# Rows of 512 tokens for the normed pair and y, and the second block's product of p ahead of its gate

## The chip, the cores and the metric

The kernel is one program on one core of a Trainium2 chip. The metric is the device time of one execution in microseconds (us), lower is better. TensorE multiplies, VectorE and ScalarE do the elementwise work, GpSimd a little of it, SyncE's queue issues nearly all loads of weights.

## The reference

Three model blocks in sequence act on 512 tokens of 1024 features (the first block on 528, since 16 meta tokens stand in front). Cut to the part that is written in another order, the end of the second block, and to the shape that most of the program has, a normed x times a weight:

```python
        hf = rmsnorm(x, norm_ffn[i])
        up = causal_dwconv(hf @ w_up[i], ffn_dw_w[i], ffn_dw_b[i])
        gate, val = jnp.split(up, 2, axis=-1)
        x = x + (jax.nn.gelu(gate) * val) @ w_down[i]

        pg = jax.nn.sigmoid(rmsnorm(x, norm_ple[i]) @ w_ple_gate[i])
        x = x + pg * (p[i] @ w_ple[i])
    return rmsnorm(x, norm_final)
```

p has 256 features per token; w_ple_gate is 1024 by 1024, w_ple 256 by 1024.

## The kernel before

Features lie on the 128 partitions, tokens along the row, so a tensor of 1024 features is 8 tiles of [128, tokens]. Products are in single precision by way of pairs: a tensor is split into a high part, rounded to the matmul's format, and the rest, the low part. One tile of a weight (128 by 128) times one tile of x takes three matmuls at L278: whi by x_hi, whi by x_lo, wlo by x_hi, with 512 columns each, and a weight load of 128 columns ahead of each.

`chain` runs a list of `Job`s, a product each, over weight slabs of up to 8 tiles. For slab s SyncE's queue loads `wbuf`, ScalarE makes `whi` (L297), VectorE subtracts to `wlo` (L395), TensorE multiplies (L278); with `ring=3` there are three buffers of each. A slab's load waits until the slab three earlier was subtracted, and ScalarE's copy waits until TensorE has used that one. Each engine takes its instructions in the order in which they are written. In turn s ScalarE and VectorE first make the slab s + 2 and then evict the tile that ended with slab s (`evict`). Norms are folded in: where a job has a `fold`, its eviction also writes the normed pair of the new x (`folded`: L315 high part, L428 low part) and squares of x (L318, L322); where two norms follow each other, both sums of squares are kept, and GpSimd adds them up (L241). The scale of a normed product is applied at its eviction, after the statistics of the sums (two matmuls with ones, a square root, a reciprocal).

The normed pair `h` is two tensors of 8 rows of T1 = 528 tokens (2112 bytes a row). The first block's projections read all 528 tokens (`rwkv_project` L679 and `qkv` L1440, in halves of 264 columns; the gates' 512 late tokens at L278). Everything later uses `half_pair`, 512 tokens of each row of 528. y, the output of the first block's recurrence, has rows of 528 too. Other operands of L278 (`gates`, `arena`, `u_hi`, `u_lo`, `o`) have rows of 512 tokens, 2048 bytes.

The second block ends with a chain of three jobs: `ffn_down_2` (kind "add", 22 tiles of weights for each of 8 output tiles, in slabs of 7, 7 and 8), `ple_gate_2` (kind "sigmoid", 8 output tiles of one slab of 8), `ple_2` (kind "sum", 8 output tiles of one slab of 2 tiles, so 6 matmuls each; its fold writes the third block's pair with both norms). Ahead of it runs the chain of `ffn_up_2`, after it the first chain of the third block.

Of the kernel before, what the change touches and what calls it, by code (L numbers as in the profile page):

```python
# [58 lines left out]
class Job:  # L59
# [3 lines left out]
    def __init__(self, w, x, kind, dst=None, gate=None, other=None, raw=None, source=None, scaled=False, fold=None):  # L63
# [46 lines left out]
def chain(nc, ones, jobs, T, norm, pending=None, ring=4, side=None, loads=(), taps=None, restore=None, ahead=None,  # L110
# [12 lines left out]
    for j, n in tiles_:  # L123
# [3 lines left out]
        sig_no.append((sig_no[-1] if sig_no else 0) + (job.kind == "sigmoid" and job.scaled))  # L127
        value_no.append((value_no[-1] if value_no else 0) + (job.kind in ("sum", "join") or (job.kind == "ffn" and n % 2 == 1)))
# [42 lines left out]
    with stage(nc) as s_:  # L171
# [35 lines left out]
        with nc.Block() as block:  # L207
# [82 lines left out]
            def _(act):  # L290
# [33 lines left out]
                def evict(s, t):  # L324
# [5 lines left out]
                    elif job.kind == "sigmoid":  # L330
                        act.wait_ge(evicted_d, by_dve[t])
                        copy(job.dst[n], job.dst[n], ACT.Sigmoid).then_inc(sig_done, 1)
                    elif job.kind == "join":
# [17 lines left out]
                    elif job.fold is not None:  # L351
                        act.wait_ge(*((value, value_no[t]) if job.kind == "sum" else (evicted_d, by_dve[t])))
# [36 lines left out]
            def _(dve):  # L389
# [47 lines left out]
                def evict(s, t):  # L437
# [16 lines left out]
                    elif job.kind in ("sum", "join"):  # L454
# [15 lines left out]
                    if job.fold is not None:  # L470
                        last = first[j] + job.N * len(job.groups)
                        if job.kind == "sum" and n > 0:
                            folded(job.fold, n - 1, job.dst[n - 1], last)
                        if job.kind != "sum" or n == job.N - 1:
                            folded(job.fold, n, job.dst[n], last)
# [370 lines left out]
def rwkv_tiles(nc, c, y, fac_scr, early, chunk_decay):  # L846
# [10 lines left out]
    with stage(nc) as s:  # L857
# [48 lines left out]
        with nc.Block() as block:  # L906
# [296 lines left out]
            def _(dve):  # L1203
# [73 lines left out]
                def outputs(i):  # L1277
                    dve.wait_ge(sr_copied, i + 1)
                    yv = y[:, i, RM:T1].rearrange("p (w a t) -> p w a t", w=W, a=2)
# [40 lines left out]
class HeadsNorm:  # L1320
# [14 lines left out]
    def pe_mean(self, pe, i):  # L1335
        if i < 8:
            if i > 0:
                pe.wait_ge(self.cen_ready, i)
            self.nc.tensor.matmul(self.mean[:], self.c["mean64"][:], self.y[:, i, T1 - T2:T1], start=True, stop=True).then_inc(self.mean_ready, 1)
# [35 lines left out]
    def dve(self, dve, t):  # L1375
        TT, TS, STT = self.nc.vector.tensor_tensor, self.nc.vector.tensor_scalar, self.nc.vector.scalar_tensor_tensor
        i, cen, var, y = t // 3, self.cen, self.var, self.y[:, t // 3, T1 - T2:T1]
# [2008 lines left out]

def half_pair(h):

    return tuple([part[:, k, 0:T2] for k in range(8)] for part in h)
# [19 lines left out]
def first_block(nc, a, x, h, ones_ident, both, far, near, norm, ahead, to_next, second):  # L3409
# [8 lines left out]
    with ExitStack() as m:  # L3418
        c = {**a, **ones_ident, **{n: resident(nc, m, n, a[n].shape) for n in CONSTANTS[1]}}
        y, y_lo = overlaid(nc, m, "y", [P, 8, T1])  # L3420
        mp = m.enter_context(ExitStack())
        p_next = mp.enter_context(nc.sbuf_tensor("p_next", [P, 3, T1], F32, side="right"))
        with ExitStack() as m2:
            decay = resident(nc, m2, "chunk_decay", [P, 8, RN + 1])
            early = y[:, 2:8, :].rearrange("p k t -> p (k t)")[:, 0:5 * (RM + 48 + RN * RC)].rearrange("p (f t) -> p f t", f=5)
            with ExitStack() as m3:
                first = resident(nc, m3, "first", [P, 8, P])
                opening(nc, a, c, both, x, h, far, near, first)
                rwkv_project(nc, c, a["w_rwkv_1"], a["w_qkv_1"], p_next, first, h, factors, early, decay, bonus, gate)
            rwkv_tiles(nc, c, y, factors, early, decay)  # L3430
        o, o_lo = overlaid(nc, m, "o", [P, 8, T2])
        with ExitStack() as m2:
            p = tile_list(p_next) + tile_list(act(m2, "p", 21))
            qkv(nc, a["w_qkv_1"][3:], h, p[3:], HeadsNorm(nc, c, y, bonus, gate))
            diff_attention(nc, c, p, o, a["subln_1"], h[0][:, 0, :], ahead, a["w_gates_1"])
        mp.close()
        late = slice(T1 - T2, T1)
        y, y_lo, o, o_lo, x = (tile_list(ap) for ap in (y[:, :, late], y_lo[:, :, late], o, o_lo, x[:, :, late]))
# [5 lines left out]
        jobs = [Job(a["w_gates_1"], tuple(tile_list(part[:, :, late]) for part in h), "sigmoid", dst=gates),  # L3444
# [10 lines left out]
def second_block(nc, a, x, h, ones_ident, far, near, kept, linear, norm, ahead, pending, to_next, second):  # L3455
# [8 lines left out]
    with ExitStack() as m:  # L3464
# [33 lines left out]
        plain, u_hi = (tile_list(t) for t in overlaid(nc, m, "u_hi", [P, 22, T2]))  # L3498
        u = (u_hi, high(m, "u_lo", 22))
        with ExitStack() as m1:  # L3500
            p, p_lo = overlaid(nc, m1, "p", [P, 2, T2])
            chain(nc, ones, [Job(a["ffn_up_2"], now, "ffn", dst=u, scaled=True)], T2, norm, ahead=ahead.take(), following=a["ffn_down_2"], pending=to_ffn, ring=3, taps=c["ffn_taps"],
                  loads=[(p[:], a["p_2"])])
# [4 lines left out]
            ple_gate, p_pair, ps = plain[0:8], (u_hi[8:10], tile_list(p_lo)), tile_list(p)  # L3508
# [5 lines left out]
    return third  # L3514


def third_block(nc, a, x, h, ones_ident, early, kept, linear, norm, ahead, pending, out):

    norms, xs, now = ones_ident["norms"], tile_list(x), half_pair(h)
# [3 lines left out]
    with ExitStack() as m:  # L3523
        branches = [overlaid(nc, m, name, [P, 4, T2]) for name in ("o_m", "o_l", "o_d")]
        o_m, o_l, o_d = (plain for plain, _ in branches)
# [27 lines left out]
        parts = [tile_list(plain) for plain, _ in branches]  # L3553
        pairs = [(rounded[24 + 4 * (n % 2):28 + 4 * (n % 2)], tile_list(low)) for n, (_, low) in enumerate(branches)]
# [11 lines left out]
def program(nc, a, out):  # L3566

    with ExitStack() as memory:
        common = {n: resident(nc, memory, n, a[n].shape) for n in CONSTANTS[0]}
        x, h = resident(nc, memory, "x", [P, 8, T1]), resident_pair(nc, memory, "h", [P, 8, T1])  # L3570
# [7 lines left out]
        to_third = Fold(half_pair(h), both[:, 1, :], 1e-6, norms[:, INNER[1], :], 1e-6)  # L3578
        far = nc.dram_tensor("bias_by_distance", (8, P, 640), F32).ap()
        near = nc.dram_tensor("bias_by_residue", (8, 16, 62), F32).ap()  # L3580
        kept, linear = ExitStack(), ExitStack()
# [176 lines left out]
```

## Time and profile before

| what | us |
|---|---|
| median of 3 runs (3595.03, 3599.8, 3618.14) | 3599.8 |
| the profiled execution, its own time | 3602.74 |
| its span | 3600.9 |
| TensorE busy (93% of the span) | 3335.8 |
| VectorE busy (55%) | 1968.1 |
| ScalarE busy (35%) | 1273.7 |
| GpSimd busy (10%) | 369.9 |

The mean granted TensorE clock is 0.953 of full speed. Start times are in us from the span's start. A matmul's record lasts about 0.39 us and overlaps the next one's; how often one starts is read from the count in a stretch.

### The profile page before, as it was taken

How to read it: one execution, taken by the hardware profiler on the slowest of the kernel's cores; microseconds unless marked ns; L12 is line 12 of the kernel's file. 1: busy time of each engine (PE TensorE's matmuls, PEld its weight loads, DVE VectorE, ACT ScalarE, POOL GpSimd, SP SyncE). 2: the span in 40 equal slices, each digit the busy share in tenths (PEclk: the TensorE clock that was granted, in tenths of full speed). 3: DMA queues.
4: the chain of work that ended last, by engine and by line, in shares of the span. 5: the costliest groups of instructions: out<-in, count | busy, mean ns of one | idle time of the engine just before them, and what ended most of it. 6: DMA issues, size and time to landing. Idle time of an engine off the chain costs nothing. (4 is left out here: it accounts for less than half of the span.)

```text
span 3600.9 us, 57034 instructions
## 1 busy us (share of the span) xinstructions
PE 3335.8 (93%) x24148; PEld 2744.3 (76%) x24148; DVE 1968.1 (55%) x3021; ACT 1273.7 (35%) x2188; POOL 369.9 (10%) x292
## 2 busy tenths in 40 slices
PE   7998999999999999889999999979599889999998
PEld 6987988866888888666777887857587587878886
DVE  4985564565355344486545775356736545464343
ACT  4552323255334233215433443234312324333232
POOL 2322230020000001009300000020100020000000
PEclk9998998999999999998999999989799799999999
DMA  4432112201222222420122222312022003232221
GB/s 150 149 133 69 35 33 101 71 7 50 97 92 95 95 94 89 130 76 27 48 85 93 98 94 92 107 63 77 12 95 85 1 2 117 76 105 100 94 94 65
DMA packets 99317, 287.83 MB, mean 80 GB/s; under 512 B 19594, under 2 KB 23818, under 8 KB 97016
## 3 DMA queue, kind: packets, MB, share of 16 engines
q1 hardware_dynamic: 92528, 269.27, 22.5%
q10 hardware_dynamic: 6536, 14.91, 1.6%
q8 instruction: 192, 3.15, 0.4%
q14 instruction: 61, 0.50, 0.0%
HBM read 264.22 MB, written 19.89 MB: 79 GB/s over the span
## 5 line engine op out<-in xcount | busy, mean ns | idle before, releaser
L278 PE MATMUL acc<-h_hi,whi 128*128 128x512 f32 x1992 | 796.5, 400 | 48.4 <-DVE wlo L505 36.5
L278 PE MATMUL acc<-h_hi,wlo 128*128 128x512 f32 x1992 | 790.6, 397 | 0.0
L278 PE MATMUL acc<-h_lo,whi 128*128 128x512 f32 x1928 | 769.2, 399 | 0.0
L278 PEld LDWEIGHTS acc<-h_hi,whi 128*128 128x128 f32 x1992 | 378.9, 190 | 147.8 <-DVE wlo L505 38.7
L395 DVE TENSOR_TENSOR wlo<-wbuf,whi 128x1024 fp32r<-128x1024 f32 (+3 forms) x277 | 321.8, 1162 | 276.2 <-ACT whi L297 273.7
L278 PEld LDWEIGHTS acc<-h_hi,wlo 128*128 128x128 f32 x1992 | 378.9, 190 | 87.1
L278 PEld LDWEIGHTS acc<-h_lo,whi 128*128 128x128 f32 x1928 | 366.3, 190 | 87.8 <-issue 2.9
L297 ACT ACTIVATE whi<-wbuf 128x1024 fp32r<-128x1024 f32 (+3 forms) x277 | 274.4, 991 | 315.6 <-PE acc L278 290.2
L278 PE MATMUL acc<-arena_round,whi 128*128 128x512 f32 x736 | 236.7, 392 | 4.8 <-DVE arena_round L461 4.8
L395 DVE TENSOR_TENSOR wlo<-ahead,whi 128x1024 fp32r<-128x1024 f32 (+3 forms) x132 | 154.6, 1171 | 140.6 <-ACT whi L297 139.9
L297 ACT ACTIVATE whi<-ahead 128x1024 fp32r<-128x1024 f32 (+3 forms) x132 | 131.4, 995 | 172.0 <-PE acc L278 166.5
L241 POOL TENSOR_TENSOR sums<-sums,sqx 128x512 f32<-128x512 f32 x28 | 38.6, 1400 | 1273.4 <-ACT sqx L318 1273.4
L278 PEld LDWEIGHTS acc<-arena_round,whi 128*128 128x128 f32 x736 | 139.4, 190 | 34.9 <-DVE arena_round L461 5.6
L278 PE MATMUL acc<-arena_round,wlo 128*128 128x512 f32 x416 | 162.9, 391 | 0.0
L679 PE MATMUL acc<-h_hi,whi 128*128 128x264 f32 x480 | 141.2, 294 | 7.5 <-POOL wlo L667 7.5
L278 PE MATMUL acc<-gates_round,whi 128*128 128x512 f32 x384 | 140.0, 392 | 3.0 <-DVE gates_round L461 1.8
L467 DVE TENSOR_TENSOR x<-acc,x 128x512 f32<-128x512 f32 x64 | 44.2, 691 | 175.2 <-PE acc L278 175.2
L679 PE MATMUL acc<-h_lo,whi 128*128 128x264 f32 x480 | 136.8, 285 | 0.0
L679 PE MATMUL acc<-h_hi,wlo 128*128 128x264 f32 x480 | 136.8, 285 | 0.0
L278 PE MATMUL acc<-gates_round,wlo 128*128 128x512 f32 x320 | 124.9, 390 | 0.0
L338 ACT ACTIVATE val<-tmp 128x512 f32<-128x512 f32 x64 | 40.5, 633 | 216.6 <-DVE tmp L463 216.6
L1440 PE MATMUL acc<-h_hi,whi 128*128 128x264 f32 x336 | 102.8, 306 | 2.5 <-DVE wlo L1480 2.5
(764 smaller groups left out, 6412.5 us busy)
## 6 DMA issues: line engine op xcount, KB each, us to landing
wbuf<-in_mlp_out SPq DMA_DIRECT2D x46, 512.0 KB, 3.3
wbuf<-in_mlp_in SPq DMA_DIRECT2D x45, 512.0 KB, 3.2
wbuf<-in_w_gates SPq DMA_DIRECT2D x38, 512.0 KB, 3.3
wbuf<-in_ffn_up SPq DMA_DIRECT2D x29, 512.0 KB, 3.2
wbuf<-in_w_qkv SPq DMA_DIRECT2D x22, 512.0 KB, 3.4
rwkv_factors<-factors SPq DMA_DIRECT2D x8, 1320.0 KB, 4.6
ahead<-in_mlp_in SPq DMA_DIRECT2D x19, 512.0 KB, 3.3
wbuf<-in_w_rwkv SPq DMA_DIRECT2D x18, 512.0 KB, 5.6
```

What stands on the lines that cost most here:

```text
L241: nc.gpsimd.tensor_tensor(sums[q][:], sums[q][:], sqx[q][:], ALU.add).then_inc(both_summed, 1)
L278: mm = nc.tensor.matmul(acc[t % NB][:, 0:T], wt[s % ring][:, k - a, :], xt, start=(kx == 0 and q == 0), stop=(kx == job.K - 1 and q == 2))
L297: copy(whi[s % ring][:, 0:size(s), :], wbuf[s % ring][:, 0:size(s), :], ACT.Copy).then_inc(hi_ready, 1)
L338: copy(val[t % 2][:], tmp[t % 2][:], ACT.Square)
L395: TT(wlo[s % ring][:, 0:size(s), :], wbuf[s % ring][:, 0:size(s), :], whi[s % ring][:, 0:size(s), :].bitcast(F32), ALU.subtract).then_inc( ...
L467: TT(job.dst[n], ps, job.other[n], ALU.add).then_inc(evicted_d, 1)
L679: mm = nc.tensor.matmul(acc[n % 2][:, hf, 0:H], wt[n % R][:, kx, :], xt[:, kx, at], start=(kx == 0 and q == 0), stop=(kx == 7 and q == 2))
L1440: mm = nc.tensor.matmul(acc[n % NB][:, h, 0:H], wt[n % R][:, k, :], xt[:, k, h * H:(h + 1) * H], start=(k == 0 and q == 0), stop=(k == 7 a ...
```

## The change

1. **Rows.** `NormedPair` lays out each part of the pair twice over the same bytes: `by_meta`, rows of 528 for the first block's projections, and `late`, rows of 512. y has rows of 512. The pads of the two tensors make both parts' late rows start at byte 480 modulo 2048, and what is allocated behind them moves along. The third block gets a pair of its own (`third_pair`, first 16 rows of the u tensor), and its three branch outputs lie where h was.
2. **Order.** The chain that ends the second block runs `ple_2` first (kind "copy", ScalarE evicts to `from_p`), then `ffn_down_2`, then `ple_gate_2` with a new kind "gated": VectorE scales the tile, ScalarE takes the sigmoid, VectorE multiplies with `from_p` and adds x, and the fold follows. The kind "sum" with a fold is no longer used.

Starts of the operands of L278 as they are allocated, in bytes modulo 2048, high part / low part:

| operand pair | before | after |
|---|---|---|
| half pair h, rows 0 to 7 | 1952, 2016, 32, ... 352 / 416, 480, ... 864 | 480 / 480 |
| late tokens of `by_meta` (gates of the first block) | 2016, 32, ... / 480, 544, ... | 2016, 32, ... / 544, 608, ... |
| y | 1504 / 1056, 1120, ... 1504 | 480 / 480 |
| diff_out (h row, o) | 1952, 2016, ... / 1504 | 480 / 480 |
| u | 992 / 992 | 480 / 480 |
| arena (third MLP, w_out) | 992 / 992 | 480 / 480 |
| arena by o_m, o_l, o_d | 992 / 992 | 480 / 1952 |
| attention output of the second block | 1472 / 736 | 960 / 736 |
| conv, joined gates of the second block | 1472 / 1472 | 960 / 960 |

```diff
+class NormedPair:
+    def __init__(self, nc, memory):
...
+        names = ((f"h_hi_{nc.next_id()}", 8 * T1 + 16), (f"h_lo_{nc.next_id()}", 8 * T1 + 368))
+        flat = [memory.enter_context(nc.sbuf_tensor(name, [P, n], F32R)) for name, n in names]
+        self.by_meta = tuple(t[:, 0:8 * T1].rearrange("p (k t) -> p k t", t=T1) for t in flat)
+        starts = (144, 0)
+        self.late = tuple(t[:, at:at + 8 * T2].rearrange("p (k t) -> p k t", t=T2) for t, at in zip(flat, starts))
...
-    return tuple([part[:, k, 0:T2] for k in range(8)] for part in h)
+    return tuple([part[:, k, :] for k in range(8)] for part in h.late)
...
-        y, y_lo = overlaid(nc, m, "y", [P, 8, T1])
+        y, y_lo = overlaid(nc, m, "y", [P, 8, T2])
...
+                    elif job.kind == "gated":
+                        act.wait_ge(evicted_d, by_dve[t])
+                        copy(job.temps[n % 2], job.temps[n % 2], ACT.Sigmoid).then_inc(sig_done, 1)
+                        act.wait_ge(value, value_no[t])
+                        folded(job.fold, n, job.dst[n])
...
+                    elif job.kind == "gated":
+                        v = job.temps[n % 2]
+                        TT(v, ps, scale[:], ALU.mult).then_inc(evicted_d, 1)
+                        dve.wait_ge(sig_done, sig_no[t])
+                        seq(TT(v, v, job.gate[n], ALU.mult))
+                        TT(job.dst[n], v, job.other[n], ALU.add).then_inc(value, 1)
...
-            chain(nc, ones, [Job(a["ffn_down_2"], u, "add", dst=xs, other=xs, fold=to_ple),
-                             Job(a["ple_gate_2"], now, "sigmoid", dst=ple_gate, scaled=True, source=0),
-                             Job(a["ple_2"], p_pair, "sum", dst=xs, gate=ple_gate, other=xs, raw=ps, fold=to_next)], T2, norm, ahead=ahead.take(), following=a["w_mlstm_3"][16:18], ring=3,
+            from_p = tile_list(act(m1, "from_p", 8))
...
+            chain(nc, ones, [Job(a["ple_2"], (now[0][0:2], tile_list(p_lo)), "copy", dst=from_p, raw=tile_list(p)),
+                             Job(a["ffn_down_2"], u, "add", dst=xs, other=xs, fold=to_ple),
+                             Job(a["ple_gate_2"], now, "gated", dst=xs, gate=from_p, other=xs, scaled=True, source=1, fold=to_next, temps=tile_list(plain)[0:2])], T2, norm, ahead=ahead.take(), following=a["w_mlstm_3"][16:18], ring=3,
```

ScalarE at the start of the chain that ends the second block: before, pieces of the first slab of `ffn_down_2` and the next slabs.

```order
L357 ACTIVATE whi<-ahead 128x128
L357 ACTIVATE whi<-ahead 128x256 x3
L297 ACTIVATE whi<-wbuf 128x896
L297 ACTIVATE whi<-wbuf 128x1024
L297 ACTIVATE whi<-ahead 128x896
```

Now (the changed kernel's lines): two pieces of the first slab of `ple_2`, each with a split of p, and the evictions of `ple_2` between the slabs.

```order
L363 ACTIVATE whi<-ahead 128x128
L301 ACTIVATE h_hi<-p_plain 128x512
L363 ACTIVATE whi<-ahead 128x128
L301 ACTIVATE h_hi<-p_plain 128x512
L298 ACTIVATE whi<-wbuf 128x256 x2
L330 ACTIVATE from_p<-acc 128x512
L298 ACTIVATE whi<-ahead 128x256
L330 ACTIVATE from_p<-acc 128x512
```

Two splits and eight evictions have come ahead of `ffn_down_2`. ScalarE in the middle of `ple_gate_2`: before, a sigmoid and the next slab's high part by turns.

```order
L332 ACTIVATE u_hi_plain<-u_hi_plain 128x512
L297 ACTIVATE whi<-ahead 128x1024
L332 ACTIVATE u_hi_plain<-u_hi_plain 128x512
L297 ACTIVATE whi<-wbuf 128x1024
L332 ACTIVATE u_hi_plain<-u_hi_plain 128x512
```

Now:

```order
L336 ACTIVATE u_plain<-u_plain 128x512
L316 ACTIVATE third_pair_round<-x,both 128x512
L319 ACTIVATE sqx<-x 128x512
L323 ACTIVATE sqx<-x,norms 128x512
L298 ACTIVATE whi<-ahead 128x1024
L336 ACTIVATE u_plain<-u_plain 128x512
```

The high part of slab n + 3 stands behind the whole fold of tile n. VectorE at the same place: before,

```order
L395 TENSOR_TENSOR wlo<-ahead,whi 128x1024
L451 TENSOR_TENSOR u_hi_plain<-acc,scale 128x512
L395 TENSOR_TENSOR wlo<-wbuf,whi 128x1024
L451 TENSOR_TENSOR u_hi_plain<-acc,scale 128x512
L395 TENSOR_TENSOR wlo<-wbuf,whi 128x1024
```

and now:

```order
L401 TENSOR_TENSOR wlo<-ahead,whi 128x1024
L470 TENSOR_TENSOR u_plain<-acc,scale 128x512
L472 TENSOR_TENSOR u_plain<-u_plain,from_p 128x512
L473 TENSOR_TENSOR x<-u_plain,x 128x512
L434 SCALAR_TENSOR_TENSOR third_pair_round<-x,both,third_pair_round 128x512
L401 TENSOR_TENSOR wlo<-wbuf,whi 128x1024
```

Three instructions of the eviction have moved here from `ple_2`, each behind the low part of a slab of 8 tiles where before it stood behind one of 2.

## Rows read from the trace of the kernel before

**Rows 1.** The page, 40 slices of 90 us: TensorE's busy tenths, its granted clock.

```profile
PE   7998999999999999889999999979599889999998
...
PEclk9998998999999999998999999989799799999999
```

**Rows 2.** Windows, L278's matmuls: stretch, us, PE busy (count), clock, DMA share, GB/s.

```profile
961.90:1006.50 44.60, 44.60 (x193) 1.00 0.29 96
1006.50:1051.20 44.70, 44.70 (x193) 1.00 0.26 84
1185.55:1273.65 88.10, 88.10 (x385) 1.00 0.31 102
1273.65:1362.65 89.00, 89.00 (x385) 1.00 0.27 90
1858.15:1880.55 22.40, 22.40 (x97) 1.00 0.29 84
...
3112.20:3177.50 65.30, 65.30 (x290) 1.00 0.33 101
3318.80:3405.95 87.15, 87.15 (x386) 1.00 0.30 102
```

**Rows 3.** Timeline of PE, `ple_2` and the step to the third block: start, us, what.

```profile
2394.29 0.77 PE L278 MATMUL acc<-u_hi_round,whi 128*128 128x512 f32 x1 [2.92 <-DVE wlo L395]
...
2417.89 0.79 PE L278 MATMUL acc<-h_hi,whi 128*128 128x512 f32 x1 [12.65 <-DVE wlo L505]
```

**Rows 4.** Timeline of DVE, one tile of `ple_2`.

```profile
2393.47 0.67 DVE L395 TENSOR_TENSOR wlo<-wbuf,whi 128x256 fp32r<-128x256 f32 x1 [1.56 <-ACT whi L297]
2394.07 0.68 DVE L455 TENSOR_TENSOR tmp<-acc,u_hi_plain 128x512 f32<-128x512 f32 x1
2394.78 1.05 DVE L458 TENSOR_TENSOR x<-tmp,x 128x512 f32<-128x512 f32 x1
```

**Rows 5.** Timeline of ACT, the same tile.

```profile
2395.86 0.72 ACT L315 ACTIVATE h_hi<-x,both 128x512 fp32r<-128x512 f32 x1 [2.42 <-DVE x L458]
2396.49 0.61 ACT L318 ACTIVATE sqx<-x 128x512 f32<-128x512 f32 x1
2397.01 0.71 ACT L322 ACTIVATE sqx<-x,norms 128x512 f32<-128x512 f32 x1
2397.62 0.40 ACT L297 ACTIVATE whi<-wbuf 128x256 fp32r<-128x256 f32 x1
```

**Rows 6.** Timeline of POOL, the next sums and the last.

```profile
2397.18 2.69 POOL L241 TENSOR_TENSOR sums<-sums,sqx 128x512 f32<-128x512 f32 x2 [1.90 <-ACT sqx L318]
...
2406.37 9.66 POOL L241 TENSOR_TENSOR sums<-sums,sqx 128x512 f32<-128x512 f32 x6 [1.90 <-ACT sqx L318]
```

**Rows 7.** Timeline of DVE, first tiles of `ple_gate_2`, which TensorE begins at 2333.7.

```profile
2345.14 0.69 DVE L451 TENSOR_TENSOR u_hi_plain<-acc,scale 128x512 f32<-128x512 f32 x1
2347.48 1.23 DVE L395 TENSOR_TENSOR wlo<-ahead,whi 128x1024 fp32r<-128x1024 f32 x1 [1.65 <-ACT whi L297]
2348.62 0.68 DVE L451 TENSOR_TENSOR u_hi_plain<-acc,scale 128x512 f32<-128x512 f32 x1
```

**Rows 8.** Timeline of ACT at the same tiles, and a split of p.

```profile
2345.87 0.63 ACT L332 ACTIVATE u_hi_plain<-u_hi_plain 128x512 f32<-128x512 f32 x1 [2.90 <-DVE u_hi_plain L451]
2346.41 1.04 ACT L297 ACTIVATE whi<-ahead 128x1024 fp32r<-128x1024 f32 x1
...
2375.23 0.62 ACT L300 ACTIVATE u_hi_round<-p_plain 128x512 fp32r<-128x512 f32 x1
```

**Rows 9.** Timeline of PE, the step from `ffn_up_2` to `ffn_down_2`.

```profile
2203.39 0.40 PE L278 MATMUL acc<-h_hi,wlo 128*128 128x512 f32 x1
2211.09 0.79 PE L278 MATMUL acc<-u_hi_round,whi 128*128 128x512 f32 x1 [7.31 <-DVE wlo L505]
2211.68 0.63 PE L278 MATMUL acc<-u_lo,whi 128*128 128x512 f32 x1
2212.11 0.63 PE L278 MATMUL acc<-u_hi_round,wlo 128*128 128x512 f32 x1
```

More of the change, by code:

```diff
@@ L59, with __init__ @@
 class Job:
-    def __init__(self, w, x, kind, dst=None, gate=None, other=None, raw=None, source=None, scaled=False, fold=None):
+    def __init__(self, w, x, kind, dst=None, gate=None, other=None, raw=None, source=None, scaled=False, fold=None, temps=None):
+        self.temps = temps
         self.w, self.x, self.kind, self.dst, self.gate, self.other = w, x, kind, dst, gate, other
@@ L126, in chain @@
         by_dve.append((by_dve[-1] if by_dve else 0) + (not job.by_scalar()))
-        sig_no.append((sig_no[-1] if sig_no else 0) + (job.kind == "sigmoid" and job.scaled))
-        value_no.append((value_no[-1] if value_no else 0) + (job.kind in ("sum", "join") or (job.kind == "ffn" and n % 2 == 1)))
+        sig_no.append((sig_no[-1] if sig_no else 0) + (job.kind == "sigmoid" and job.scaled or job.kind == "gated"))
+        value_no.append((value_no[-1] if value_no else 0) + (job.kind in ("sum", "join", "gated") or (job.kind == "ffn" and n % 2 == 1)))
     split_at, part, made = {}, {}, 0
@@ L351, in evict @@
                     elif job.fold is not None:
-                        act.wait_ge(*((value, value_no[t]) if job.kind == "sum" else (evicted_d, by_dve[t])))
+                        act.wait_ge(evicted_d, by_dve[t])
                         folded(job.fold, n, job.dst[n])
@@ L471, in evict @@
                         last = first[j] + job.N * len(job.groups)
[L472 removed]
+                        if job.kind == "gated" and n > 0:
                             folded(job.fold, n - 1, job.dst[n - 1], last)
[L474 removed]
+                        if job.kind != "gated" or n == job.N - 1:
                             folded(job.fold, n, job.dst[n], last)
@@ L3443, in first_block @@
         to_mlp = Fold(now, norms[:, MLP[0], :], 1e-5)
-        jobs = [Job(a["w_gates_1"], tuple(tile_list(part[:, :, late]) for part in h), "sigmoid", dst=gates),
+        jobs = [Job(a["w_gates_1"], tuple(tile_list(part[:, :, late]) for part in h.by_meta), "sigmoid", dst=gates),
                 Job(a["rwkv_out_1"], y_pair, "gate", dst=gates[0:8], gate=gates[0:8], raw=y),
@@ L3497, in second_block @@
                              Job(a["w_out_2"], joined, "add", dst=xs, other=xs, source=2, fold=to_ffn)], T2, norm, ahead=ahead.take(), following=a["ffn_up_2"], ring=3, side=ConvNorm(nc, c, conv))
-        plain, u_hi = (tile_list(t) for t in overlaid(nc, m, "u_hi", [P, 22, T2]))
-        u = (u_hi, high(m, "u_lo", 22))
+        _, third_pair = overlaid(nc, handed, "third_pair", [P, 16, T2])
+        plain, rest = overlaid(nc, m, "u", [P, 28, T2])
+        u = tile_list(third_pair) + tile_list(rest)
+        u, next_pair = (u[0:22], u[22:44]), (u[0:8], u[8:16])
+        to_next = Fold(next_pair, to_next, 1e-6, norms[:, INNER[1], :], 1e-6)
         with ExitStack() as m1:
             p, p_lo = overlaid(nc, m1, "p", [P, 2, T2])
-            chain(nc, ones, [Job(a["ffn_up_2"], now, "ffn", dst=u, scaled=True)], T2, norm, ahead=ahead.take(), following=a["ffn_down_2"], pending=to_ffn, ring=3, taps=c["ffn_taps"],
+            chain(nc, ones, [Job(a["ffn_up_2"], now, "ffn", dst=u, scaled=True)], T2, norm, ahead=ahead.take(), following=a["ple_2"], pending=to_ffn, ring=3, taps=c["ffn_taps"],
                   loads=[(p[:], a["p_2"])])
@@ L3523, in third_block @@
     with ExitStack() as m:
-        branches = [overlaid(nc, m, name, [P, 4, T2]) for name in ("o_m", "o_l", "o_d")]
-        o_m, o_l, o_d = (plain for plain, _ in branches)
+        m.enter_context(handed)
+        o_m, o_l, o_d = h.plain
         ones = ones_ident["ones"]
```

44 lines of the change are left out of this document (24 added, 20 removed).

## The prediction

> **What bounds the kernel now.** I read the page first: TensorE is busy nine tenths or more in most of the 40 slices, at full granted clock there; the slices below that are the first block's recurrence, the attentions and the joints between chains [rows 1]. So a chain of products costs what its matmuls cost, one behind the other, and I looked next at how far apart they start. The windows give it: the count in a stretch includes one or two records still running at its start, so 385 stands for 384 started. With the half pair as operand, 384 matmuls take 89.00 us, 231.8 ns each; with both parts in rows of 512 that start at one place (arena), 384 take 87.15 us, 226.9 ns; another such job has 288 in 65.30, 226.7 ns; where slabs by y's rows of 528 alternate with slabs by o's rows of 512, it is 88.10 / 384 = 229.4 ns; y's own jobs 44.60 / 192 = 232.3, the h row with o 44.70 / 192 = 232.8 [rows 2]. All of these are 512 columns at full clock, without an idle gap and with the same weight loads. What differs is the address of the moving rows. Rows of 512 tokens alone don't do it: the second block's attention output has them in both parts, one at 1472 and one at 736 modulo 2048, and takes 22.40 / 96 = 233.3 ns [rows 2]. What the fast jobs share is that all rows of both parts start at one place modulo 2048.
>
> The other place is the second block's end. In `ple_2` TensorE waits for the low part ahead of five of the eight slabs, 2.92 us in the row shown, for 6 matmuls of 0.23 each, and after the last it idles 12.65 us [rows 3]. The timelines say why: low part, eviction, add on VectorE; then h_hi, two squares and the next high part on ScalarE; then the next low part: one ring through two ordered engines, 4.6 us long (from 2393.47 to the next low part at 2398.05, 0.43 behind the high part's start at 2397.62) [rows 4, 5]. Behind it GpSimd needs 2.69 per tile, and six of its sums, 9.66 us, are left at the end [rows 6].
>
> **Part 1, the rows.** Jobs with the half pair alone: 768 matmuls of the first MLP's input, 456 and 384 of the second block's input and gates, 1056 of `ffn_up_2`, 1776 of the third block's inputs and gates, 768 of its MLP: 5208, of which I take 120 off for starts at half clock and waits. 5088 x (231.8 - 226.9) = 24.9 us. y's two jobs and the one of h and o: 576 x (232.5 - 226.9) = 3.2. The first MLP's output, 768 x (229.4 - 226.9) = 1.9. The three jobs of o_m, o_l, o_d get their parts at 480 and 1952, which differ: 288 x (about 231.8 - 226.7) = 1.4 lost. Sum: **28.6 us saved**, all on the path, since TensorE has no gap in these stretches. VectorE and ScalarE, at 55% and 35%, cover the quicker pace. No row shows a whole job at 480: the nearest are 992, 1472 and 1504, and I take the arena's value, since 992 and 1504 are 480 plus a multiple of 512. If only half of the gain comes, as in the job of alternating slabs (229.4), it is 14 us; at 226.7 it is 30. The first block's 2448 matmuls of 264 columns and its 384 gates keep rows of 528, but the low part shifts by 64 bytes against the high part. Unequal places stay unequal: I take zero, and as bounds plus and minus the 4.9 ns scaled by 264 / 512, some 6 us. The products u, arena and hidden keep equal places: zero.
>
> The Trainium skill speaks against this part: the page TensorE: Matmul & The Clock Gate, section Back-to-back issue gap, gives the gap between isolated warm matmuls as columns / 2.4 + 2.5 ns, 216 ns for 512, with no term for the moving operand's address. By that rule part 1 would be worth nothing. The rows disagree: 226.9 and 231.8 ns for one shape at one clock [rows 2]. I go by the rows and keep the rule as a rival.
>
> **Part 2, the order.** At the front, the old first matmul of `ffn_down_2` stands 7.7 us behind the last of `ffn_up_2`, and starts at half clock (0.43 us from one to the next) [rows 9]. Now `ple_2` starts there, behind one split of p (0.62 on ScalarE [rows 8], 0.7 on VectorE, which overlap the slab's pieces in part): 1.1 us later. The half-clock start falls on it instead of on `ffn_down_2`: no term. Its 48 matmuls at 0.227 are 10.9. Its evictions are single copies on ScalarE, so the next low part follows a slab's end by about 0.1 + 0.6 + 0.4 + 0.5 = 1.6 us, under the two slabs (2.7 us) that TensorE has in hand; at the first wide slab of `ffn_down_2` that is 0.1 + 0.6 + 1.0 + 1.1 = 2.8, so some 0.4 is lost. **12.4 us added** (to 14, if that slab's load is late).
>
> At the back, `ple_gate_2` takes over the ring. Tile n's low part of slab n + 2 to the next: scale to sigmoid 0.73 (2345.14 to 2345.87) [rows 7, 8], sigmoid to product 0.68, product to add 0.71 [rows 4], add to h_hi 0.73, then 0.63, 0.52 and 0.61 to the high part [rows 5], high to low part 1.07, low part to next scaling 1.14 [rows 7, 8]: 6.8 us. TensorE needs 24 x 0.227 = 5.4 for a slab. So the ring sets the pace again, as it did in `ple_2`; the wait is moved, not gone. GpSimd adds to it: its sums run from 0.7 to 3.4 us behind the first square [rows 5, 6], the wide low part starts 2.2 behind it, and VectorE's subtraction of 256 columns took 0.67 in such a shadow and the add 1.05 [rows 4] against 0.69 for the like of it without [rows 7]. I add 0.6: 7.4 us, with bounds 6.8 (no shadow) and 8.0.
>
> The Trainium skill, SBUF — State Buffer, section on the two separate sides, says of the port pair that VectorE and GpSimd share that the loser fully blocks for the other's whole instruction. By that rule the low part would wait for the end of the second sum, 1.2 us, a ring of 8.0 and 2 us less gain. The rows show less than a whole block: the add began at 2394.78, lasted 1.05 and so lost 0.4 [rows 4].
>
> From the first matmul of `ple_gate_2` as zero: slabs 0 to 2 are ready and end at 17.2 (with the statistics' two matmuls); the first eviction waits for the statistics, 2345.1 - 2333.7 = 11.4 [rows 7]; the following ones come at 18.1 (no sums yet), 25.5, 32.9, 40.3, 47.7, and slab n + 2 starts with eviction n. The last slab runs from 47.8 to 53.2. No slab is left to make, so the last two evictions follow at 51.3 and 55.9; the last squares at 59.9 and 60.4, GpSimd's last pair until 63.3. Before, GpSimd ended at 2416.0 and the third block's first matmul came 1.9 later [rows 3, 6]: so at 65.2 now, against 2417.9 - 2333.7 = 84.2 before. **19.0 us saved**; net of the front, **6.6**. The gate's share of part 1 (192 matmuls) is hidden under the ring and isn't counted. Bounds of the net: 4 with a ring of 8.0, 9 with 6.8.
>
> Sum: 3602.7 - 28.6 - 6.6 = 3567.5 for the profiled execution, whose own time lies 2.9 above the median; 3599.8 - 35.2 gives **3565**, 0.98% less. About 1% is what a measurement of this kernel can tell from no change, and the forecast sits on that line. Its own range, with the bounds above, is 3555 to 3577.
>
> **Rivals.** (a) The gated ring keeps TensorE's pace, because the engines overlap more than I credit: the slabs end at 44.4, the last sum at about 53, and part 2 saves 30 - 12 = 18; 3553. For it: the sums leave GpSimd free half of the time. Against: the order, where high and low part stand behind the fold. (b) The reorder gives nothing: with gaps of 2 us TensorE's clock falls, as it did in `ple_2` after a gap of 2.92, where matmuls lasted 0.63 [rows 3]; two slabs at half clock cost 2 x 24 x 0.2 = 10 us; 3575. (c) The change doesn't do what it says: places don't matter and the difference has another cause, such as the engine that writes the row. Part 2 alone is left, 3593. Against it is one job whose slabs alternate. (d) Slower: what counts is the absolute place, and 480 is a bad one, like the pair 1472 and 736 with 233.3. Then 1872 matmuls of hidden rows and u, fast before, lose 6.5 each (12 us), the pair's 5088 lose 1.5 (8), o_m to o_d 1.4; with part 2, 3599.8 + 21 - 7 = 3614. It decides from a pace of about 231 at 480; at 236, with the first block's halves at their bound (6 more), it passes 3636. Against it: three places, and all fast when equal.
>
> **How the numbers follow.** Forecast 0.64, half of it on either side of the line; (a) 0.11; (b) 0.10; (c) 0.08; (d) 0.07, of which 0.04 over 1%. So faster by over 1%: 0.32 + 0.11 = 0.43; within: 0.32 + 0.10 + 0.08 + 0.03 = 0.53; slower 0.04. The range leaves (c), (d) and the ends of (a) and (b) out: 3552 to 3580.
>
> **What would show it.** In the changed kernel's windows: 227 ns per matmul in `ffn_up_2`, both MLPs and the third block's gates (231.8 refutes part 1); 231 or more for o_m to o_d; `ple_2` in one run of 48 matmuls with hardly a wait; in `ple_gate_2` from the fourth slab on a wait of about 2 us per tile on the low part, behind evictions 7.4 apart; the step to the third block about 12 us as before, of which GpSimd's last sums are the end. Wrong would make it above all the pace at 480, then the ring.

## The result and the profile after

On the first chip the changed kernel took 3581.3 us (median of 7 runs, 3573.2 to 3587.1), the kernel before 3597.5 (7 runs): ratio 0.9943, interval 0.9923 to 0.9963. On two other chips it was 0.9925 (0.9908 to 0.9941) and 0.9927 (0.9909 to 0.9944). One run of the kernel before on the second chip took 9309.7 us and is left out of its ratio. So the change is faster by 0.57 to 0.75%, 20 to 27 us (16 by the two medians above), where 35 were forecast. 3581.3 lies 1.3 above the range of 3552 to 3580 and 4.3 above the narrower 3555 to 3577; as a ratio, 0.9943 against the 0.9945 that 3580 is of 3599.8, it falls just inside the wider one, as do the medians of the other two chips (3577.7, 3579.3). The profiled execution took 3574.1, 28.6 below the profiled one of before.

The page of the kernel after shows TensorE as busy as before in nearly all slices; the picture of [rows 1] is the same, with the stages a little earlier:

```profile
PE   7997999999999999888999999979599899999998
...
PEclk9998998999999999998999999999799789999999
```

The windows that answer to [rows 2], in the same order of jobs (y's first, h with o, the first MLP's output and second input, attention output, o_m to o_d, the third MLP's output). Line 278 of the kernel before is L279 here. A count includes the one or two matmuls still running at the start; 192, 384, 96 and 288 start in the windows:

```profile
958.45:1002.00 43.55, 43.55 (x194) 1.00 0.28 98
1002.00:1045.50 43.50, 43.50 (x194) 1.00 0.25 85
1177.00:1264.05 87.05, 87.05 (x386) 1.00 0.30 104
1264.05:1351.10 87.05, 87.05 (x386) 1.00 0.27 92
1843.55:1865.75 22.20, 22.20 (x98) 1.00 0.29 86
3087.85:3153.80 65.95, 65.95 (x290) 1.00 0.32 101
3292.35:3379.40 87.05, 87.05 (x386) 1.00 0.29 102
```

The MLP's input fell from 89.00 to 87.05, 226.7 ns per matmul; y's job, the one of h and o, and the MLP's output came to 226.6 to 226.8 as well; o_m to o_d rose from 65.30 to 65.95 (229.0). So far the direction of every term holds. The forecast does not hold in other jobs that read the same pair. Stretches inside `w_in_2`, `gates_2` and `w_gdn_3`, of before and then of after, in which the pair is the only moving operand:

```profile
1510.00:1550.00 40.00, 40.00 (x173) 1.00 0.74 188
1815.00:1855.00 40.00, 40.00 (x174) 1.00 0.21 70
2620.00:2680.00 60.00, 60.00 (x261) 1.00 0.28 93
```

```profile
1500.00:1540.00 40.00, 40.00 (x173) 1.00 0.72 191
1800.00:1840.00 40.00, 40.00 (x173) 1.00 0.21 70
2600.00:2660.00 60.00, 60.00 (x263) 1.00 0.28 95
```

At 226.7 ns, 40 us hold 176 or more. The first two jobs gained nothing, the third less than half.

In the second block's end, `ple_2` runs in one piece behind its first half-clock matmuls and `ple_gate_2` takes over the ring. Timeline of PE after, as [rows 3] and [rows 9]: last matmul of `ffn_up_2`, first of `ple_2`, first of `ple_gate_2`, one of the waits in it, first of the third block:

```profile
2183.95 0.39 PE L279 MATMUL acc<-h_hi,wlo 128*128 128x512 f32 x1
2192.66 0.76 PE L279 MATMUL acc<-h_hi,whi 128*128 128x512 f32 x1 [8.32 <-DVE p_round L406]
...
2326.30 0.39 PE L279 MATMUL acc<-h_hi,whi 128*128 128x512 f32 x1
...
2360.18 0.47 PE L279 MATMUL acc<-h_hi,whi 128*128 128x512 f32 x1 [1.96 <-DVE wlo L401]
...
2393.61 0.79 PE L279 MATMUL acc<-third_pair_round,whi 128*128 128x512 f32 x1 [12.34 <-DVE wlo L517]
```

Timeline of DVE there (compare [rows 7]) and of POOL (compare [rows 6]), evictions on line 470, low parts of weight slabs on line 401:

```profile
2337.75 0.69 DVE L470 TENSOR_TENSOR u_plain<-acc,scale 128x512 f32<-128x512 f32 x1 [0.20 <-DVE scale L422]
...
2343.44 1.23 DVE L401 TENSOR_TENSOR wlo<-wbuf,whi 128x1024 fp32r<-128x1024 f32 x1 [2.88 <-ACT whi L298]
2344.58 0.68 DVE L470 TENSOR_TENSOR u_plain<-acc,scale 128x512 f32<-128x512 f32 x1
...
2350.26 2.09 DVE L401 TENSOR_TENSOR wlo<-ahead,whi 128x1024 fp32r<-128x1024 f32 x1 [2.21 <-ACT whi L298]
2352.27 0.68 DVE L470 TENSOR_TENSOR u_plain<-acc,scale 128x512 f32<-128x512 f32 x1
```

```profile
2348.74 2.52 POOL L242 TENSOR_TENSOR sums<-sums,sqx 128x512 f32<-128x512 f32 x2 [621.22 <-ACT sqx L319]
```

The first turn of the ring, with no sum beside it, took 2344.58 - 2337.75 = 6.83: the 6.8 of the prediction. With GpSimd's sums from 2348.74 on, the low part took 2.09 in place of 1.23 and the next turn 7.69.

### The profile page after: what moved, and what is told of

It is laid out like the page before. It is cut to its first block and busy times, and to the rows that moved or that the text cites. A ratio compares the mean times of both kernels' runs of the same rounds, so it can differ in the third digit from the quotient of the medians.

```text
span 3572.3 us, 57041 instructions
## 1 busy us (share of the span) xinstructions
PE 3312.0 (93%) x24148; PEld 2742.7 (77%) x24148; DVE 1965.4 (55%) x3019; ACT 1278.1 (36%) x2194; POOL 367.0 (10%) x292
## 5 line engine op out<-in xcount | busy, mean ns | idle before, releaser
L279 PE MATMUL acc<-third_pair_round,whi 128*128 128x512 f32 x1824 | 584.6, 396 | 24.1 <-DVE wlo L517 20.4
L279 PE MATMUL acc<-h_hi,whi 128*128 128x512 f32 x1160 | 463.0, 399 | 39.8 <-DVE wlo L517 16.1
L279 PE MATMUL acc<-h_hi,wlo 128*128 128x512 f32 x1160 | 458.7, 395 | 0.0
L279 PE MATMUL acc<-h_lo,whi 128*128 128x512 f32 x1080 | 426.5, 395 | 0.0
L279 PEld LDWEIGHTS acc<-third_pair_round,whi 128*128 128x128 f32 x1824 | 345.5, 190 | 104.7 <-DVE wlo L517 21.2
L279 PE MATMUL acc<-third_pair_round,wlo 128*128 128x512 f32 x976 | 383.3, 393 | 0.0
L279 PEld LDWEIGHTS acc<-h_hi,whi 128*128 128x128 f32 x1160 | 221.0, 190 | 94.4 <-issue 21.5
L279 PEld LDWEIGHTS acc<-h_hi,wlo 128*128 128x128 f32 x1160 | 220.8, 190 | 49.5
L279 PEld LDWEIGHTS acc<-h_lo,whi 128*128 128x128 f32 x1080 | 205.3, 190 | 46.3 <-issue 1.4
L279 PE MATMUL acc<-arena_round,whi 128*128 128x512 f32 x736 | 236.0, 392 | 4.6 <-DVE arena_round L467 4.6
L279 PEld LDWEIGHTS acc<-third_pair_round,wlo 128*128 128x128 f32 x976 | 185.1, 190 | 40.8
L279 PEld LDWEIGHTS acc<-arena_round,whi 128*128 128x128 f32 x736 | 138.9, 189 | 34.6 <-DVE arena_round L467 5.4
L279 PE MATMUL acc<-arena_round,wlo 128*128 128x512 f32 x416 | 162.5, 391 | 0.0
L279 PE MATMUL acc<-gates_round,whi 128*128 128x512 f32 x384 | 140.3, 393 | 3.0 <-DVE gates_round L467 1.8
```

Source lines behind the costliest of these rows:

```text
L279: mm = nc.tensor.matmul(acc[t % NB][:, 0:T], wt[s % ring][:, k - a, :], xt, start=(kx == 0 and q == 0), stop=(kx == job.K - 1 and q == 2))
```

## Theories

Two things are to be told apart. First, why `ffn_up_2` and the MLPs reached 226.7 and `gates_2` did not, with the same rows. What differs between them in the addresses that the programs allocate is the weight: the tiles `whi` and `wlo` that TensorE loads. They lie 512 bytes apart in their buffers, so within a chain their place is the same modulo 512. In `ffn_up_2` and both MLPs it is 480, like the rows'; in `w_in_2` 320, in `gates_2` 448, in the third block's first projections 32, in `w_gdn_3` and `w_mlstm_3` 160. In the kernel before, each fast job had its weights at the place of its rows too (1504 and 992 are 480 modulo 512), so the two readings could not be separated there. **Theory:** a matmul is fast where its moving row and its weight tiles start at the same place modulo some power of two. **Rivals:** equal rows of both parts suffice, and the slow jobs have another cause (the reading on record); or 480 is a good place by itself. Second, what the new order alone is worth, and whether its ring is what limits it.

## The experiments

**The rows without the order, and the changed kernel beside it.** `rows_only` is the kernel before with the pair and y in their new rows, and the old order of the second block:

```diff
-        y, y_lo = overlaid(nc, m, "y", [P, 8, T1])
+        y, y_lo = overlaid(nc, m, "y", [P, 8, T2])
...
-        x, h = resident(nc, memory, "x", [P, 8, T1]), resident_pair(nc, memory, "h", [P, 8, T1])
+        x, h = resident(nc, memory, "x", [P, 8, T1]), NormedPair(nc, memory)
```

> Part 1 of the change alone: the pair, y and their users in rows of 512 at 480, and the order of the products as before (ffn_down, ple_gate, ple_2); o_m, o_l, o_d stay in whole rows at one place (480). Theory of the record, places count by themselves: every job with the pair at 226.7 to 227 ns per matmul; 30 us less than before (28.6 and the 1.4 that o_m to o_d no longer lose), ratio 0.992. Theory now, the moving rows must stand at the place of the weight tiles modulo 512 bytes: 226.7 in both MLPs, ffn_up and the third block's gates, but 233 to 234 in w_in_2 (weights at 832 modulo 2048), gates_2 (960) and the third block's first projections (544), 229 in w_gdn and w_mlstm; 16 to 18 us less than before, ratio 0.9955. Rival, the gain is the order's and the clock's: no difference from before. The order alone is the changed kernel against this one: by the record 5 us in the changed kernel's favour (6.6 less 1.4), by the rival that the reorder gives nothing 0 or less; the joint with the old order shows 12 to 13 us from ple_2's last matmul and five waits of some 3 us in ple_2.

> The changed kernel unchanged, beside before and the part alone on one chip: ratio 0.993 to 0.996 by the runs so far (3573 to 3587 us). If the spread of its runs follows the granted clock in the third block's scans, as the two profiles say (0.72 and 0.86 granted over 110 us there), runs at 0.955 take 3573 and runs at 0.951 some 3586; if the spread has another cause, time and clock don't go together.

Measured: `rows_only` 3582.5 us, ratio 0.9934 (0.9918 to 0.995); the changed kernel 3577.7, 0.9925 (0.9908 to 0.9941), both against 3607.2. The rows carry nearly all of it: 24.7 us by medians, between the two theories (16 to 18, and 30), so this run does not decide between them. The order is worth 3 to 5 us by the medians, less than the intervals can separate; the profile measures it better. Timeline of PE of `rows_only`, as [rows 9] and [rows 3] (last of `ffn_up_2`, first of `ffn_down_2`, first of `ple_gate_2`, a wait in `ple_2`, first of the third block):

```profile
2194.29 0.39 PE L278 MATMUL acc<-h_hi,wlo 128*128 128x512 f32 x1
2201.99 0.79 PE L278 MATMUL acc<-u_hi_round,whi 128*128 128x512 f32 x1 [7.31 <-DVE wlo L505]
...
2323.36 0.39 PE L278 MATMUL acc<-h_hi,whi 128*128 128x512 f32 x1
...
2378.49 0.47 PE L278 MATMUL acc<-u_hi_round,whi 128*128 128x512 f32 x1 [2.62 <-DVE wlo L395]
...
2406.68 0.80 PE L278 MATMUL acc<-h_hi,whi 128*128 128x512 f32 x1 [12.19 <-DVE wlo L505]
```

From `ffn_up_2`'s last matmul to `ple_gate_2`'s first: 129.1 us here, 142.3 in the changed kernel, 13.3 more at the front. From there to the third block: 83.3 here, 67.3 there, 16.0 less at the back. Net 2.7. Part of the 13.3 is not the order's: `rows_only` started `ffn_down_2` with 7 matmuls at half clock (0.43 us from one to the next), where the profiles of the kernel before and of the changed one show 13 at the start of this chain. Against the kernel before, 2203.39 [rows 9] to 2333.7 [rows 7], the front cost 12.0. Time and clock go together in the changed kernel's six runs (3575 at 0.954, 3589.7 at 0.951), though 3586.5 came at 0.950.

**The pair moved away from its weights.** `pair_128` puts the pair 128 bytes further and leaves everything else; `all_128` moves what is behind along:

```diff
 # pair_128
-        names = ((f"h_hi_{nc.next_id()}", 8 * T1 + 16), (f"h_lo_{nc.next_id()}", 8 * T1 + 368))
+        names = ((f"h_hi_{nc.next_id()}", 8 * T1 + 48), (f"h_lo_{nc.next_id()}", 8 * T1 + 336))
-        starts = (144, 0)
+        starts = (176, 0)
 # all_128: as pair_128, but
+        names = ((f"h_hi_{nc.next_id()}", 8 * T1 + 48), (f"h_lo_{nc.next_id()}", 8 * T1 + 368))
```

> The changed kernel with the pair 128 bytes further (608 modulo 2048, both parts, rows still of 512), and everything behind it where it was: the weight tiles of these jobs stay at 480. Theory now (rows must match the weight tiles modulo 512): mlp_in_1 and ffn_up go from 226.7 to 231 or more ns per matmul, 1824 x 5 to 7 = 9 to 13 us more; the third block's gates and MLP, whose pair is another buffer at 480, stay at 226.7. Theory of the record (equal rows are enough, at any place): 226.7 in all of them, and no difference from the changed kernel. Third: 608 is a bad place by itself: slow here, and slow in the run in which the weights move along.

> The same pair at 608, with everything behind it moved by 128 bytes too: the weight tiles of the MLPs, ffn_up and the gates of the third block are at 608, as are y, hidden, u and arena. Theory now: 226.7 ns again in mlp_in_1, ffn_up, the third block's gates and MLP, the same time as the changed kernel but for attn_out, one of whose parts stays at 736. Third theory, 608 bad by itself: 231 or more in all of these, 7000 matmuls x 5 = 35 us more. The record's theory: as the changed kernel.

Windows of L279's matmuls in `pair_128` (second input of the first MLP, 384; inside `ffn_up_2`; second input of the third MLP, 384), then in `all_128` (the first two):

```profile
1273.85:1363.45 89.60, 89.60 (x386) 1.00 0.27 89
1960.00:2200.00 240.00, 239.70 (x1031) 1.00 0.28 92
3396.80:3483.85 87.05, 87.05 (x386) 1.00 0.28 91
```

```profile
1270.15:1357.20 87.05, 87.05 (x386) 1.00 0.29 91
1960.00:2200.00 240.00, 239.00 (x1051) 1.00 0.28 93
```

With rows at 608 and weights at 480, 89.60 / 384 = 233.3 ns, slower than the uneven rows of the kernel before (231.8); `ffn_up_2` likewise. The third block, whose pair did not move, kept 226.7. With the weights at 608 too, the first MLP's job is at 226.7 again and `ffn_up_2` has 20 matmuls more in its 240 us. Both rivals fall: equal rows alone do not suffice, and one place, 608, is slow or fast by where the weights stand. The whole executions (3591.5 and 3589.2, one each) say nothing beside scatter of that size.

**Which modulus.** `pair_256` moves the pair 256 bytes from its weights (names + 80 and + 304, starts 208).

> The changed kernel with the pair 256 bytes further (736 modulo 2048), the weight tiles where they were (480). If places count modulo 512 bytes: 231 to 234 ns per matmul in mlp_in_1 and ffn_up, as with 128 bytes (233.3 and 232.4). If they count modulo 256: 226.7, the changed kernel's pace. w_in_2, whose weights then stand 96 bytes from the pair, and gates_2 (224) show what other distances cost; so far 160 and 32 cost 7 and 6.5 ns, 192 cost 2.

The same job, and inside `ffn_up_2`:

```profile
1268.50:1355.55 87.05, 87.05 (x386) 1.00 0.28 91
1960.00:2190.00 230.00, 230.00 (x1017) 1.00 0.27 90
```

226.7 ns, although the rows stand at 736 and the weights at 480. So the places count modulo 256 bytes, not 512 or 2048: my expectation's "modulo 512" was too strict. No smaller power of two will do, since 128 bytes apart was slow. The second block's `o_lo` at 736 beside weights at 448 modulo 512 is a mismatch by this rule as well, which fits the 233.3 of the attention output in [rows 2] that I had put down to unequal parts.

**Weights at the rows' place in every chain.** `matched` adds gaps until all weights of this matmul (L281 there) start at 480 modulo 512, and o_m to o_d at 2016:

```diff
+        if pad:
+            s_.sb("pad", [P, pad])
         wbuf = [s_.sb("wbuf", [P, wide, P]) if ahead is None or i else ahead[0] for i in range(ring)]
...
+            resident(nc, m1, "gap", [P, 8])
             glu = resident(nc, m1, "glu", [P, 4, CONV_TAPS - 1 + T2])
 # pad (4-byte words): 32 for w_in_2, 112 for the third block's first chain, 80 for w_gdn_3; 16 ahead of o_m
```

> The changed kernel with unused gaps that put the weight tiles of every chain at 480 modulo 512 bytes, the place of the pair (before: 320 in w_in_2, 448 in gates_2 and its chain, 32 in the third block's first projections, 160 in w_gdn and w_mlstm), and o_m to o_d at 2016 in place of 1952 (480 modulo 512). Theory of the relative place: 226.7 to 227 ns per matmul in gates_2 (now 233.3: 384 x 6.4 = 2.5 us), w_in_2 (now 233.8, of its 456 those that nothing else holds up: up to 2.9), the third block's small and GLA projections (233: 432 x 6 = 2.6), w_gdn and w_mlstm (229: 768 x 2.2 = 1.7), the up jobs (228.9: 288 x 2.2 = 0.6): together 8 to 10 us less than the changed kernel, ratio against before 0.990. Rival, equal rows of both parts are all that can be had and those jobs are slow for another reason (their weights come late, their evictions): no matmul gap changes, ratio 0.9925 as the changed kernel on this chip.

Measured: 3569.4 us, 0.9901 (0.988 to 0.9921). Stretches inside `w_in_2`, `gates_2` and `w_gdn_3`, then the attention output (96) and o_m to o_d (288):

```profile
1498.50:1538.50 40.00, 40.00 (x177) 1.00 0.80 178
1800.00:1840.00 40.00, 40.00 (x178) 1.00 0.21 66
2600.00:2660.00 60.00, 60.00 (x266) 1.00 0.30 97
1842.30:1864.05 21.75, 21.75 (x98) 1.00 0.32 87
3079.70:3144.95 65.25, 65.25 (x290) 1.00 0.35 102
```

173 became 177 and 178, 263 became 266, 22.20 us became 21.75 and 65.95 became 65.25: the theory's pace in each. The rival that those jobs were slow for a reason of their own falls.

**The ring.** `late_fold` lets ScalarE fold tile n - 1 behind the sigmoid of tile n, so that no weight slab's high part waits for the tile's own product and add:

```diff
                         copy(job.temps[n % 2], job.temps[n % 2], ACT.Sigmoid).then_inc(sig_done, 1)
-                        act.wait_ge(value, value_no[t])
-                        folded(job.fold, n, job.dst[n])
+                        for done in range(max(0, n - 1), n + 1 if n == job.N - 1 else n):
+                            act.wait_ge(value, value_no[t - n + done])
+                            folded(job.fold, done, job.dst[done])
```

> The changed kernel, with ScalarE's fold of a tile of the gated product one tile later: it scales tile n - 1 and squares it after the sigmoid of tile n, so that the next weight slab's high part no longer stands behind the wait for the tile's own product and add. If the ring of the record sets the pace in ple_gate (7.4 forecast, 7.7 between the evictions of the changed kernel): the ring becomes scaling 0.7, sigmoid 0.7, fold 1.8, high part 1.1, low part 1.1 = 5.4, TensorE's own pace, the waits of some 2.3 us ahead of the last slabs go, and the joint from ple_gate's first matmul to the third block's falls from 67 to 59 or 60 us: 7 to 8 less than the changed kernel. Rival, GpSimd's sums (2.7 per tile) or VectorE's work (3.9 per tile) hold it: at most 2 less, the waits stay.

> Both edits together: the weight tiles at the pair's place in every chain, and the fold one tile late. Theory: they touch different stages and add up, 15 to 18 us less than the changed kernel, ratio against before about 0.988. Rival: one is lost to the other or to the granted clock in the scans behind it, ratio 0.990 or more.

Measured: `late_fold` 3574.8, 0.9919 (0.9897 to 0.994); `matched_late` 3569.4, 0.989 (0.9864 to 0.9915), against 3569.4 and 0.9901 of `matched`. The stage did what was expected, the medians showed next to nothing of it, and the changed kernel had run on another chip. So all three were run again on one chip, with the kernel before for a second profile:

> The changed kernel, on one chip with the two below, since the late fold and the changed kernel stood on different chips so far (0.9919 and 0.9925 of before, 7.7 us apart in the profiles' stage of the gate, and within 2 us in the medians). Expected from the runs so far: 0.9925 of before, medians between 3577 and 3581 us; the scans ahead of gates_1 between 869 and 875 us and the second block's attention between 179 and 188, as the granted clock falls there.

> The late fold again, beside the changed kernel on the same chip. If the 7.7 us that its stage is shorter reach the end: 6 to 9 us below the changed kernel's median here. If they are lost behind the stage, to a lower granted clock in the scans of the third block: no difference, and the third block from w_mlstm to the last matmul longer by as much in the profile.

> Weight tiles at the pair's place in every chain and the late fold, beside both on one chip: if the two add up, 15 to 18 us below the changed kernel, 0.988 of before; if the late fold brings nothing, 8 to 10 below, 0.990.

> The kernel before, for a second profile. Between the last matmul of the mLSTM input and the third block's gates it had 186.1 us, every kernel with the changed rows 189.5 to 191.6, with a lower granted clock there (0.85, 0.70, 0.95 over thirds against 0.81, 0.64, 0.92). If this stretch is a property of the kernel before: 186 again. If it was chance of one execution: 190 to 192 here too. The joint in the second block again: 84.2 us from ple_gate's first matmul to the third block's first, 231.7 ns per matmul in ffn_up.

Measured: the changed kernel 3579.3, 0.9927 (0.9909 to 0.9944); the late fold 3572.7, 0.9904 (0.9886 to 0.9921); both edits 3565.1, 0.9877 (0.9857 to 0.9897). By the medians the late fold brings 6.6 and both edits 14.2, a little under the 15 to 18 expected if they add up. The stage itself is sure: 59.7 us in all four profiles with the late fold, 67.3 to 67.4 in all three of the changed kernel. That its gain reaches the end is likely, not shown: the intervals of the late fold and the changed kernel overlap, and on the other chip both edits and `matched` alone stood at the same 3569.4. Both edits together are faster than the changed kernel: their interval ends at 0.9897, its begins at 0.9909.

In the late fold's second run the stage is as short as expected, from 2327.47 to 2387.19 on PE, 59.7 us. But the timelines of PE, DVE and POOL show that the ring is not what I expected:

```profile
2327.47 0.39 PE L279 MATMUL acc<-h_hi,whi 128*128 128x512 f32 x1
...
2361.58 0.47 PE L279 MATMUL acc<-h_hi,whi 128*128 128x512 f32 x1 [0.38 <-DVE wlo L402]
...
2368.26 0.47 PE L279 MATMUL acc<-h_hi,whi 128*128 128x512 f32 x1 [0.97 <-DVE wlo L402]
...
2387.19 1.22 PE L279 MATMUL acc<-third_pair_round,whi 128*128 128x512 f32 x2 [13.21 <-DVE wlo L518]
```

```profile
2345.50 0.75 DVE L435 SCALAR_TENSOR_TENSOR third_pair_round<-x,both,third_pair_round 128x512 fp32r<-128x512 f32 x1
...
2354.69 0.68 DVE L471 TENSOR_TENSOR u_plain<-acc,scale 128x512 f32<-128x512 f32 x1
...
2357.40 1.79 DVE L435 SCALAR_TENSOR_TENSOR third_pair_round<-x,both,third_pair_round 128x512 fp32r<-128x512 f32 x1
2359.12 2.31 DVE L402 TENSOR_TENSOR wlo<-wbuf,whi 128x1024 fp32r<-128x1024 f32 x1
2361.36 0.68 DVE L471 TENSOR_TENSOR u_plain<-acc,scale 128x512 f32<-128x512 f32 x1
```

```profile
2357.25 3.10 POOL L242 TENSOR_TENSOR sums<-sums,sqx 128x512 f32<-128x512 f32 x2 [3.56 <-ACT sqx L319]
```

Evictions are 6.67 apart, not 5.4: GpSimd's 3.10 now lie beside two of VectorE's instructions, 1.79 in place of 0.75 and 2.31 in place of 1.23. That is 2.1 us per tile, more than the 1.3 that the ring lacks to TensorE's 5.4. The stage came out all the same, since the first turns, ahead of the sums, and the last ones, with no slab to make, are shorter than 6.67, and TensorE waits only twice. What the sums would cost on another engine was not tried.

**The kernel before again** (3600.6) repeats the products: the pace of `ffn_up_2` is 230.00 us for 994 matmuls where the changed kernel has 1014:

```profile
1960.00:2190.00 230.00, 230.00 (x994) 1.00 0.28 93
```

```profile
1950.00:2180.00 230.00, 230.00 (x1014) 1.00 0.27 92
```

The stretch between the mLSTM's input and the third block's gates, 186.1 us in the first profile of before, was 189.7 now, against 189.5 to 191.7 in the changed kernels: most of that difference was chance of one execution.

## Why the prediction was right, and where it was off

Direction and place held, and the likeliest class (within 1%) came; the size was 8 to 15 us too large, in two terms. The mechanism of the rows was half of the true one. That 480 met the weights of `ffn_up_2`, both MLPs and the third block's gates was luck: I chose it for its likeness to the fast jobs' 992 and 1504 and did not know that their weights stood at the same place. Rows equal in both parts but 128 bytes off their weights gain nothing, as `pair_128` shows.

1. **The rows, 28.6 forecast.** The terms for y, o and the first MLP's output held: 1.05 + 1.2 + about 1.1 for the three jobs (3.2 forecast), 2 x 1.05 for the output (1.9); o_m to o_d lost 0.65 (1.4 forecast). The half pair did not: of 24.9, the full 5 ns came in 3168 matmuls (the first MLP's input, `ffn_up_2`, the third block's gates and MLP), 15.8 us. `w_gdn_3` and `w_mlstm_3` went to 229.0 (60 us / 262): 768 x 2.7 = 2.1. The other 1272, of `w_in_2`, `gates_2` and the third block's first projections, got nothing (in 40 us of the first two 173 and 174, now 173 each). The first block's projections, taken as zero, moved within their scatter: from the first matmul of `rwkv_project` to its last 223.9 and 225.6 us in two profiles of before, 225.2 to 226.7 in three of the changed kernel. The step that failed is the sentence "What the fast jobs share is that all rows of both parts start at one place modulo 2048." They shared a second thing, weights at that place, and this one decides: `pair_128` has the first without the second and is slow, `pair_256` and `all_128` have the second and are fast. I had read the moving operand's addresses of every fast job, and the weights' of none.
2. **The order, 6.6 forecast, 4.9 measured against before and 2.7 against `rows_only`.** The front cost 12.0 against before and 13.3 against `rows_only` (12.4 forecast): the start came 8.7 behind `ffn_up_2`, 1.0 later than before, as forecast. The back saved 16.0 against `rows_only` and 16.9 against before, where 19.0 stood. The ring's working held to a tenth without the sums (6.83 for 6.8); "I add 0.6" for GpSimd's shadow was 0.86, so 7.7 for 7.4 in each turn. The low part that began at 2350.26 stood beside two sums (2348.74 to 2351.26) and lasted 0.86 longer than its like, where I had extrapolated a partial loss from the add of [rows 4]. That row was misread: the two sums beside the add ended at 2397.18 - 1.90 = 2395.28 [rows 6], only 0.50 after it began, so its loss of 0.36 was most of what was left of them, as 0.86 of 1.00 is here. The Trainium skill, SBUF — State Buffer, section on the two separate sides, has the loser of the shared port pair block for the other's whole instruction. By that the low part would have lost the 1.00 until 2351.26, so this row lies near the rule, and the 8.0 that I gave the rule came from sums that I took to run longer.
3. **Rivals.** (c) and (d) fall with the 226.7 at 480, (a) with the waits of 1.96. The Trainium skill, TensorE: Matmul & The Clock Gate, section Back-to-back issue gap, gives a gap without a term for addresses. The runs speak against it for this stream: 226.7 and 233.3 ns for one shape at full clock. (b), a clock that falls in the gaps, did not come: matmuls behind them keep 0.47 and less.
4. **Sum by the rows:** 15.8 + 2.1 + 3.3 + 2.1 - 0.65 + 2.7 = 25 us, or 28 with the order's 4.9, against 20 to 27 measured on three chips. The 28.6 between the two profiled executions is not the better number: the stretch ahead of `w_gates_1`, whose operands the change only shifts, came out 4.2 us shorter in it (868.7 for 872.9), and between 866.5 and 876.6 in the other runs.

Left open: what in the chip makes the place matter. The load of a weight tile lasts 0.19 us in fast and slow jobs alike, so the records do not show it. Nor is the price of a mismatch fixed. In the attention output only the low part, one matmul in three, is off its weights' place, and with the same addresses in both kernels it took 22.20 us in the changed kernel and 22.40 in `pair_128`, 231.3 and 233.3 ns; o_m to o_d, with the low part alone off too, stand at 229.0, and `gates_2`, with both parts off, at 233.

```profile
1857.70:1880.10 22.40, 22.40 (x98) 1.00 0.31 84
```

## What to carry to other kernels

Where single-precision pairs are multiplied tile by tile, put the moving rows, the high and the low part, and the weight tiles at the same place modulo 256 bytes: in this kernel that was 226.7 ns per 512 columns against 229 to 234 otherwise, 1 to 3% of a product, and pads of 8 to 112 words did it. Other shapes and types were not tried. When fast and slow jobs are compared by addresses, list every operand before naming the one that counts. A term for VectorE's work beside GpSimd is read from the overlap that the new order will give: two sums cost an add 0.4 us in [rows 4], a low part 0.9 in the changed kernel, and two instructions 2.1 behind the late fold.

## What the runs showed of the hardware

The place rule above was not expected. The scatter of the runs was not either: the MLPs' jobs repeat to 0.1 us from run to run, while stretches that wait on many small steps do not. The second block's attention, from the last matmul of `w_in_2` to the first of `gates_2`, with 960 matmuls each time: the changed kernel in two profiles, then both edits together. The first number behind the stretch is its length, then the busy times of PE, PEld, DVE, ACT and POOL; the granted clock stands ahead of the last two.

```profile
1564.30:1743.00 178.70, 151.21 (x960) 111.42 (x958) 125.59 (x377) 74.61 (x271) 113.92 (x80) 0.89 0.05 14
```

```profile
1570.10:1758.30 188.20, 157.87 (x960) 114.93 (x958) 129.53 (x377) 74.61 (x271) 113.89 (x80) 0.87 0.05 13
```

```profile
1569.10:1762.80 193.70, 168.44 (x960) 123.81 (x959) 125.10 (x377) 74.93 (x271) 113.96 (x80) 0.80 0.05 13
```

From the first to the third the granted clock fell from 0.89 to 0.80, a mean of its two levels, and the stretch grew by 15 us, about as much as all of the change's gain in the half pair. The clock is not the whole of it: in the second profile it is only 0.02 lower, but VectorE's 377 instructions took 129.53 us in place of 125.59. In the changed kernel's two profiles shown, 3574.1 and 3589.7 us long, this one stretch is 9.5 of the 15.5 us between them. Why the clock differs between executions of one program was not tried.
